# One decoder layer on one core: output projection with 512 + 32 columns instead of 272 + 272 in four of eight chunks

## The reference

```python
def post_mix(h, o_a, o_b, w_out, g1, b1, g2, b2, wi2, wo2, p, ple_proj, ple_gate):
    o = jnp.concatenate([o_a.reshape(bsz, t, WIDTH_A), o_b.reshape(bsz, t, WIDTH_B)], -1).astype(h.dtype) @ w_out
    h = layer_norm(ALPHA * h + o, g1, b1)
    h = layer_norm(ALPHA * h + 0.5 * swiglu(h, wi2, wo2), g2, b2)
    return h + (p @ ple_proj) * jax.nn.sigmoid(h @ ple_gate)

# per layer, for the prompt and for the decode tokens:
#   h = pre_mix(x)                      layer_norm(alpha*x + 0.5*swiglu(x))
#   q, k, v, indexer = h @ w_in
#   o_a: three dilated windows          o_b: top-k sparse attention of an indexer
#   x = post_mix(h, o_a, o_b, w_out, ...)
```

## Time and profile before

| | |
|---|---|
| median of two runs | 1456.01 us (1454.33 and 1457.69) |
| span of the profiled execution | 1454.2 us |
| PE busy | 1376.8 us, 95% of the span |
| DVE, ACT, POOL busy | 542.2, 455.0, 615.0 us |
| output projection, first to last product of line 1611 | 902.0 to 947.3 us |
| a product of 272 columns, as recorded | 288 ns median |

### The profile page before, as it was taken

How to read it: one execution, slowest core, us unless ns; L and a number is a source line. 1 busy time by engine, 2 the same in 40 slices (tenths; PEclk the granted TensorE clock), 3 DMA queues, 4 the chain that set the end, 5 groups by cost and what they waited for, 6 DMA issues and landing times.

```text
span 1454.2 us, 30740 instructions
## 1 busy us (share of the span) xinstructions
PE 1376.8 (95%) x12059; PEld 1272.3 (87%) x12059; DVE 542.2 (37%) x1340; ACT 455.0 (31%) x841; POOL 615.0 (42%) x423
## 2 busy tenths in 40 slices
PE   7999999999989999999877897989999999999988
PEld 7899999999979879976555666979999999999888
DVE  3222222200243246788899322272222222200444
ACT  4122222211262343257544420162222222211541
POOL 3344444354465645223454004644433334453632
PEclk9999999999999999999989997989999999999989
DMA  7399765766355523332399887444656567665121
GB/s 247 114 259 320 243 211 189 271 229 210 108 181 185 150 83 104 136 113 60 105 284 282 276 298 265 149 135 149 211 189 219 181 220 255 225 218 174 57 71 45
DMA packets 96638, 269.83 MB, mean 186 GB/s; under 512 B 36401, under 2 KB 36786, under 8 KB 96280
## 3 DMA queue, kind: packets, MB, share of 16 engines
q1 hardware_dynamic: 89864, 255.34, 52.4%
q0 software_dynamic: 5632, 10.50, 2.7%
q10 hardware_dynamic: 1040, 2.62, 1.2%
HBM read 259.78 MB, written 109.10 MB: 254 GB/s over the span
## 4 chain that ended last, share of the span: by engine, by line
PE 83%; DVE 8%; POOL 3%; DMA 2%; issue 2%; ACT 2%; SPq 0%; ACTq 0%; DVEq 0%; POOLq 0%
PE bank L1611 22%; PE bank L1615 22%; PE bank L1613 22%; DMA cache_a_ring<-in_cache_a 2%; DVE idx_scores L1453 2%; POOL w_rest L577 2%; PE bank L2154 2%; PE bank L1659 2%; PE bank L1660 1%; PE bank L1661 1%; PE bank L1961 1%; PE bank L1971 1%; PE bank L1983 1%; DVE idx_scores_left L1399 1%; DVE topk_lists L1398 1%
## 5 line engine op out<-in xcount | busy, mean ns | idle before, releaser
L577 POOL TENSOR_TENSOR w_rest<-w_raw,w_high 128x1024 fp32r<-128x1024 f32 (+2 forms) x159 | 410.2, 2580 | 604.4 <-ACT w_high L744 603.4
L744 ACT ACTIVATE w_high<-w_raw 128x1024 fp32r<-128x1024 f32 (+2 forms) x159 | 180.2, 1134 | 766.9 <-PE bank L1615 733.4
L1611 PE MATMUL bank<-x_high,w_high 128*128 128x272 f32 x1808 | 377.5, 290 | 8.7 <-DVE x_rest L1021 8.7
L1615 PE MATMUL bank<-x_high,w_rest 128*128 128x272 f32 x1808 | 374.9, 289 | 0.0
L1613 PE MATMUL bank<-x_rest,w_high 128*128 128x272 f32 x1808 | 373.6, 288 | 0.0
L1611 PEld LDWEIGHTS bank<-x_high,w_high 128*128 128x128 f32 x1808 | 284.7, 189 | 15.5 <-POOL w_rest L577 8.6
L1613 PEld LDWEIGHTS bank<-x_rest,w_high 128*128 128x128 f32 x1808 | 285.0, 189 | 0.0
L1615 PEld LDWEIGHTS bank<-x_high,w_rest 128*128 128x128 f32 x1808 | 283.0, 189 | 0.0
L1053 DVE SCALAR_TENSOR_TENSOR hidden<-silu_gate,bank 128x272 f32<-128x272 f32 x88 | 34.6, 434 | 386.8 <-ACT silu_gate L764 386.8
L1611 PE MATMUL bank<-hidden_high,w_high 128*128 128x272 f32 x616 | 127.7, 288 | 0.0
L1615 PE MATMUL bank<-hidden_high,w_rest 128*128 128x272 f32 x616 | 127.5, 288 | 0.0
(11 more groups left out here) (317 smaller groups left out, 1863.1 us busy)
## 6 DMA issues: line engine op xcount, KB each, us to landing
out_a_sample<-in_cache_a SPq DMA_DIRECT2D x73, 1344.0 KB
w_raw<-in_w_wi SPq DMA_DIRECT2D x88, 512.0 KB, 5.1
cache_a_ring<-in_cache_a SPq DMA_DIRECT2D x112, 384.0 KB, 5.0
w_raw<-in_w_wo SPq DMA_DIRECT2D x32, 704.0 KB, 5.6
w_raw<-in_w_w_in SPq DMA_DIRECT2D x26, 512.0 KB, 3.6
w_raw<-in_w_gate SPq DMA_DIRECT2D x8, 640.0 KB, 3.8
bias_toeplitz<-rev_bias POOLq DMA_DIRECT2D x32, 128.0 KB, 2.7
kv_b_pages<-in_cache_b POOLq DMA_DIRECT2D x64, 64.0 KB, 4.1
```

The costliest lines, as they stand in the source:

```text
L577: nc.gpsimd.tensor_tensor(rest_part(u0, i, j)[:, 0:tiles, :], RAW[:, slot, 0:tiles, :], high_part(u0, i, j)[:, 0:tiles, :].bitcast(F32), A ...
L744: nc.scalar.activation(high_part(u0, i, j)[:, 0:tiles, :], RAW[:, slot, 0:tiles, :], ACT.Copy).then_inc(S["hi_ready"], 1)
L1611: mm(banks[n][:, 0:HALF], wh, xh[n], start=start, stop=False)
L1615: last = mm(banks[n][:, 0:HALF], wl, xh[n], start=False, stop=stop)
```

## The change

In units 0 to 3 of the output projection the two column ranges are no longer halves but kinds: the 512 prompt columns go to the first bank of the pair, which they fill, and the 32 decode columns to the second. The new `unit_by_kind` runs all eight tiles of the unit for the prompt columns (24 products of 512 columns) and then all eight again for the decode columns (24 of 32). `evacuate` reads the two banks with the same cut. Units 4 to 7 and the other stages stay as they were; the wait for the whole attention output before unit 0 stays too.

```diff
--- before.py
+++ after.py
@@ -323,6 +323,13 @@
         def half(t, k, n):
             a, b = HALVES[n]
             return t[:, k, a:b]
+
+        def kind(t, k, n):
+
+            return t[:, k, 0:SEQ] if n == 0 else t[:, k, SEQ:T]
+
+        KINDS = (SEQ, NDEC)
+        BY_KIND = 4
 
 
 
@@ -1070,9 +1077,10 @@
 
                 u0, per = FIRST[("wo1", "w_out", "wo2")[which]], (2, 1, 2)[which]
                 dve.wait_ge(S["unit_used"], u0 + per * (m + 1))
+                split, cols = (kind, KINDS) if which == 1 and m < BY_KIND else (half, (HALF, HALF))
                 for n in range(2):
-                    last = v.scalar_tensor_tensor(half(Y, m, n), half(Y, m, n), ALPHA, BANK[2 * (m % 2) + n][:, 0:HALF],
-                                                  ALU.mult, ALU.add)
+                    last = v.scalar_tensor_tensor(split(Y, m, n), split(Y, m, n), ALPHA,
+                                                  BANK[2 * (m % 2) + n][:, 0:cols[n]], ALU.mult, ALU.add)
                 return last
 
             def part_sum(which):
@@ -1629,6 +1637,18 @@
                         between(t)
                 return last
 
+            def unit_by_kind(u0, m, banks, high, low):
+
+                wh, wl = high_part(u0, m // 4, m % 4), rest_part(u0, m // 4, m % 4)
+                pe.wait_ge(S["lo_ready"], u0 + m + 1)
+                for n in range(2):
+                    out = banks[n][:, 0:KINDS[n]]
+                    for k in range(KD):
+                        mm(out, wh[:, k, :], kind(high, k, n), start=k == 0, stop=False)
+                        mm(out, wh[:, k, :], kind(low, k, n), start=False, stop=False)
+                        last = mm(out, wl[:, k, :], kind(high, k, n), start=False, stop=k == KD - 1)
+                return last
+
             def up_stage(which):
                 u0 = FIRST[("wi1", "wi2")[which]]
 
@@ -2202,6 +2222,9 @@
                 s = m % 2
                 if m >= 2:
                     pe.wait_ge(S["y_part"], PART + m - 1)
+                if m < BY_KIND:
+                    unit_by_kind(u0, m, BANK[2 * s:2 * s + 2], OH_, OL_).then_inc(S["unit_used"], 1)
+                    continue
                 unit(u0, m // 4, m % 4, BANK[2 * s:2 * s + 2], OH_, OL_, 0, KD, True, True,
                      between=mean_between if m == 6 else None).then_inc(S["unit_used"], 1)
             last_chunk(1, OH_, OL_)
```

## The result

| | before | after |
|---|---|---|
| median | 1456.01 us (1454.33 to 1457.69, 2 runs) | 1469.43 us (1468.62 to 1470.25, 2 runs) |
| span of the profiled execution | 1454.2 us | 1467.0 us |
| first to last product on the attention output | 902.0 to 956.7 us | 901.5 to 969.4 us |

The ratio is 1.010, with a 95% interval from 1.0069 to 1.0132: 13.4 us slower, clear of the noise and under 2%. In the profiled executions the difference is 12.8 us, and the output projection with its last chunk takes 67.9 us instead of 54.7, 13.2 more. So all of it lies there: ahead of it stand 901.5 us (902.0 before), behind it 497.6 (497.5 before).

A forecast was written before the change was run, and what follows sets the result against it. PE's products were taken to bound the kernel. Four chunks +7.6 us, breaks -0.24 and one clock fall +1.7 made +9.0 us: 1463.2 in the span, 1465 us as median; range 1458 to 1472 us, held with at least 0.80.

The forecast's parts named there:

- Item 2: Short products of 32 columns, 24 per chunk: their weight loads set the pace, 111 ns each, bounds 63 and 125.5.
- cheap: Rival on the short products: loads at 63 ns or partly hidden behind the product before, 1458 us; chance 0.10.
- never hidden loads: Rival: a load on all 128 rows cannot overlap a running product, so the change costs nothing, 1456 us; chance 0.03.
- products that wait for each other: Rival: short products adding into the same 32 columns each wait out the one before, 0.28 us, 1490 us; chance 0.05.
- Item 1: Long products of 512 columns, 24 per chunk: 216 ns each, 3 ns above their columns, bounds 213 and 225.5.
- if the long ones keep the 12 ns: Sign of a wrong prediction: long products carry 12 ns on top of their columns, as 272 columns did, instead of 3.
- Item 4: First chunk of the output projection, begun at half clock: 10.7 us instead of 8.6, 2.1 us more.
- Item 5: PE's two short waits for evacuations, before chunks 2 and 4: both vanish, -0.24 us.
- Item 8: Granted clock in the four chunks: one fall after a thin run of short products, +1.7 us, bounds 0 and 4 (+6.8).
- the prediction's own sign of being wrong: On the clock in the four changed chunks: the prediction is wrong if the clock falls in every chunk.

The follow-up runs named there:

- pairs: The changed kernel with each short product directly behind its long one, in chunks 0 to 3: 1488.09 us, ratio 1.0235; in chunks 1 to 4 instead: 1462.85 us.
- groups of six: The changed kernel with its products in alternating groups of 6 long and 6 short in the four chunks: 1462.81 us in the median, ratio 1.0093.

## Why the prediction was right, and where its sum was off

The forecast was +9.0 us, 1465 us; measured were +13.4 and, in the six runs of the changed kernel again, a ratio of 1.0084, which is 12 us. The range held both, and the mechanism is the one forecast: a load with nothing long to hide behind sets the pace of the short products, and the thin runs cost the clock. Two of its terms were too small, though, and the width of the range, from no fall to four, is what kept it right: with the terms of items 1 and 2 at their upper bounds alone (9.6 us) the measured +13.4 would lie outside.

- *Item 2, short products.* 111 ns forecast, 112 measured. That it goes with the width of the loaded weights and not with the streamed columns is shown by halving the weights (58 ns) and by four times the columns (still 112). The rivals with cheap or never hidden loads and with products that wait for each other are out: 112 ns is neither 25 nor 63 nor 280, and a pair of 343 ns is not the 251 of before.
- *Item 1, long products.* Mis-sized, and beyond my upper bound: 216 ns forecast, 225.5 the bound, 231 measured. I took the 3 ns on top from the plain f32 products at line 1669, since they last as long. Length in time was the wrong likeness. By the prediction's own sign (wrong "if the long ones keep the 12 ns") this item failed: they carry 18. The amount follows the columns of the reduced form (5 ns and 0.4425 ns a column), at 272, 384 and 512 alike, and it isn't there at half clock (427 ns for 512, 320 for 384). 15 ns more for the 67 long products at full clock (96 less 13 in chunk 0, and 16 under the falls behind chunks 1 and 2) are 1.0 us.
- *Item 4, chunk 0.* Forecast +2.1 us; by PE's starts 10.68 us against 8.70, +2.0. That is luck in part: the 15 ns on its long products at full clock add 0.2 us, and half clock, which lasted 5.3 us behind the first product instead of 5.8, took as much away. Where it ends differs from one execution to the next (3.2 to 6.0 us behind the first product in the profiles where long products or halves came first, but for the one held for 19).
- *Item 5, the breaks.* DVE's evacuation of chunk 0 was over at 918.18 us (917.39 and 0.79), 2.2 us before chunk 2 began at 920.41, so this break is gone, as forecast; that of chunk 2 was over at 936.16 us (935.38 and 0.78), 3.9 us before chunk 4. That is 0.2 us in all, too little for a median.
- *Item 8, the clock.* This is the larger of the two misses: one fall was forecast, three came, in both profiles of this kernel. Each cost 1.5 to 1.6 us (1.7 forecast), so 3.0 us more. The bounds of 0 and 4 held it; a fourth fall would have met the prediction's own sign of being wrong.
- Sum by measured terms: 7.6 - 0.24 + 1.0 + 4.7 + 0.1 (112 for 111 ns) = +13.2 us in the stage, and 13.2 is what the stage shows. Without falls, the kernels with short products in groups or of 128 columns show +7.7 and +8.7; these two differ in chunk 0, where half clock lasted 3.2 and 5.6 us.
- *Not foreseen*: that half clock can hold itself. Only pairs and, once in three profiles, groups of six were held by it; the two profiles of the changed kernel, whose chunks begin with 24 long products in a row, show half clock ending 4.2 and 5.3 us behind the first product. That the long row is the reason is my reading. My item on the clock had weighed only how it falls.
- The rules of the Trainium skill, "TensorE: Matmul & The Clock Gate": that a load overlaps running matmuls only in other row groups (Part 3, "The mechanism") does not hold here, neither before (125.5 ns a product) nor after: a chunk takes 8.23 us, where by that rule, with the 110 ns of a load in the earlier trace rows, 24 x (227 + 2 x 110) ns = 10.7 us is my estimate. Section "LDWEIGHTS (loading the stationary operand)" gives the columns of the weights over 1.2 as nanoseconds, 107 and 53 ns for 128 and 64: the runs at full clock agree up to 5 ns (112 and 58), those at half clock do not (213). Section "Back-to-back issue gap" gives 512 columns N/2.4 + 2.5 = 216 ns as the isolated gap; the trace does not agree, 231.

## What to carry to other kernels

A product costs at least its load: with 128x128 weights in this form, 32, 128 and 160 columns all took 112 ns. By 5 + 0.4425 ns a column that is the price of some 240, an estimate, since nothing between 160 and 272 was run. So a width that has to be cut in two is cut in the middle: 272 + 272 cost 251 ns, 384 + 160 287 and 512 + 32 343. Where short products can't be avoided, look at the granted clock behind and ahead of them, and put a dense stream first when they would meet half clock: the same 96 pairs cost 8 us or 34, by where they began. A range for such an effect needs both directions, how the clock is lost and how it comes back.

## What the runs showed of the hardware that was not expected

- Products in the reduced float32 form take 5 ns and 0.4425 ns a column at full clock (125, 175 and 231 ns for 272, 384 and 512), not 0.417 ns a column; at half clock exactly their columns at 1.2 GHz (227, 320, 427 ns). Why it is so is open; the bank is not the reason, nor the order, and no run had such products without a load of their own.
- A load of 128x128 weights takes 112 ns at full clock and 213 at half, in a stream of short products.
- Half clock held for 61.5 us under a PE that never paused: its rows show PE 61.49 of 61.50 us busy. The same pairs, begun at full clock, kept it for 33.0 us, also busy throughout, so busy time doesn't tell the two apart.
- Four times the columns in the short products made the kernel 4 us faster by the medians, 3 by the means; its profile shows no fall where that of the changed kernel shows three.
